# The first mixer's conditioning rows taken by TensorE's column quarters instead of VectorE

## The reference, cut to what matters

```
c_act = jax.nn.silu(c)
for l in range(DEPTH):
    mod = (c_act @ w_mod[l] + b_mod[l])[:, None, :]
    sh1, sc1, g1, sh2, sc2, g2 = jnp.split(mod, 6, axis=-1)
    h = x * (1.0 + sc1) + sh1
    y = hybrid_mixer(h, w_in[l], w_a2[l], b_a[l], gla_norm_g[l], w_out[l])
    ...
```

## Time and profile before

| | |
|---|---|
| median of 3 runs | 1253.62 us (1253.2 to 1255.18) |
| the profiled execution, its own time | 1260.17 us |
| its span in the trace | 1258.4 us |
| PE busy | 1157.7 us (92%) |
| DVE busy | 546.1 us (43%) |
| ACT busy | 284.2 us (23%) |
| moved by DMA | 422.69 MB, mean 336 GB/s |

### The profile page before, as it was taken

How to read it: one execution, slowest core, us unless ns; L and a number is a source line. 1 busy time by engine, 2 the same in 40 slices (tenths; PEclk the granted TensorE clock), 3 DMA queues, 4 the chain that set the end, 5 groups by cost and what they waited for, 6 DMA issues and landing times.

```text
span 1258.4 us, 25820 instructions
## 1 busy us (share of the span) xinstructions
PE 1157.7 (92%) x11004; PEld 637.1 (51%) x11004; DVE 546.1 (43%) x881; ACT 284.2 (23%) x486; POOL 62.1 (5%) x118
## 2 busy tenths in 40 slices
PE   1889679999998897799999999999999999999986
PEld 1779668778878797642333333333333333333322
DVE  6799688867767997732110110121111101210124
ACT  0556234344335654211010010010100100100100
POOL 2101100000012011010000000000000000000101
PEclk9999889999999998899999999999999999999988
DMA  9976696799855865998999999999999999999991
GB/s 342 302 254 203 224 321 221 288 336 382 277 172 159 291 220 194 382 378 315 413 412 399 410 403 407 412 396 411 411 392 412 413 389 411 412 401 411 412 390 55
DMA packets 156504, 422.69 MB, mean 336 GB/s; under 512 B 20988, under 2 KB 74656, under 8 KB 145120
## 3 DMA queue, kind: packets, MB, share of 16 engines
q1 hardware_dynamic: 146720, 395.16, 82.9%
q0 software_dynamic: 6080, 20.31, 4.6%
q10 hardware_dynamic: 3584, 5.51, 1.3%
HBM read 405.20 MB, written 15.73 MB: 334 GB/s over the span
## 4 chain that ended last, share of the span: by engine, by line
PE 66%; DMA 15%; DVE 9%; SPq 4%; issue 3%; ACT 2%; POOL 1%; DVEq 0%; ACTq 0%
PE bank L1376 33%; PE bank L1390 18%; DMA slots<-zeros 8%; PE bank L340 4%; PE bank L342 3%; PE bank L341 3%; DMA raw_w<-in_moe_w_down_dram 3%; DVE mod_acc L1543 2%; DMA raw_u<-in_ffn_w_up_dram 2%; DMA u_raw<-in_w_in_dram 2%; DVE u_low L1554 2%; PE bank L1264 1%; SPq L427 1%; SPq L379 1%; SPq L487 1%
## 5 line engine op out<-in xcount | busy, mean ns | idle before, releaser
L1376 PE MATMUL bank<-raw_w,xg 128*32 128x512 f32 (+1 forms) x4608 | 461.9, 560 | 5.0 <-DMA raw_w<-in_moe_w_up_dram 3.0
L1376 PEld LDWEIGHTS bank<-raw_w,xg 128*32 128x32 f32 x4608 | 154.4, 110 | 309.4 <-issue 301.9
L1928 DVE TENSOR_TENSOR he<-he,bank 128x256 f32<-128x256 f32 (+1 forms) x72 | 25.7, 383 | 535.6 <-ACT he L901 535.6
L1390 PE MATMUL bank<-raw_w,heT 128*32 128x512 f32 x2112 | 232.9, 596 | 3.0 <-DMA raw_w<-in_moe_w_down_dram 2.9
L1390 PEld LDWEIGHTS bank<-raw_w,heT 128*32 128x32 f32 x2112 | 72.0, 110 | 157.8 <-issue 152.9
L901 ACT ACTIVATE he<-bank 128x256 f32<-128x256 f32 (+1 forms) x72 | 21.3, 367 | 572.9 <-PE bank L1376 572.9
L1543 DVE SCALAR_TENSOR_TENSOR mod_acc<-mod_row,c_act,mod_acc 128x1024 f32<-128x1024 f32 x70 | 89.8, 1283 | 7.7 <-DMA mod_row<-in_w_mod_dram 1.5
L340 PE MATMUL bank<-u_high,hT_H 128*128 128x256 f32 x256 | 75.5, 295 | 2.3 <-DVE u_low L1554 2.3
L341 PE MATMUL bank<-u_low,hT_H 128*128 128x256 f32 x256 | 72.7, 284 | 0.0
L342 PE MATMUL bank<-u_high,hT_L 128*128 128x256 f32 x256 | 72.6, 284 | 0.0
L340 PE MATMUL bank<-gu_H,hT_H 128*128 128x512 f32 x160 | 64.8, 405 | 0.0
(11 more groups left out here) (299 smaller groups left out, 1267.0 us busy)
## 6 DMA issues: line engine op xcount, KB each, us to landing
raw_w<-in_moe_w_down_dram SPq DMA_DIRECT2D x88, 1024.0 KB, 16.8
raw_w<-in_moe_w_gate_dram SPq DMA_DIRECT2D x128, 512.0 KB, 13.1
raw_w<-in_moe_w_up_dram SPq DMA_DIRECT2D x128, 512.0 KB, 15.6
mod_row<-in_w_mod_dram SPq DMA_DIRECT2D x80, 512.0 KB, 6.2
raw_w<-in_moe_w_gate_dram SPq DMA_DIRECT2D x64, 384.0 KB, 11.7
raw_w<-in_moe_w_up_dram SPq DMA_DIRECT2D x64, 384.0 KB, 13.5
u_raw<-in_w_in_dram SPq DMA_DIRECT2D x20, 1024.0 KB, 8.2
raw_d<-in_ffn_w_down_dram SPq DMA_DIRECT2D x11, 1024.0 KB, 9.9
```

Of the source, the lines that this page charges most:

```text
L1376: last = mm(bank[g][32 * q:32 * q + 32, 0:2 * HALF[c]].rearrange("s (m j r) -> s m j r", m=2, r=64), xg[:, i, g, k, :], cols[:, :, :, 64 * ...
L1390: last = mm(bank[3 + g][32 * q:32 * q + 32, :], heT[(par + c) % 2][:, g, 2 * a + b, :], W[:, b, h * 512:(h + 1) * 512], start=(c == 0 and ...
L1928: V.tensor_tensor(h, h, bank[g][:, w:2 * w].rearrange("s (j c b) -> s j b c", b=2, c=32), ALU.mult).then_inc(s["m_hid"], 1)
```

## The change

The eight-step accumulation on DVE goes. ACT makes `c_wide`, where each of the 8 values of `silu(c)` on a partition stands 32 times side by side. For each tile PE makes two products: `c_wide[:, k]` (128 x 32) is the stationary side, one half of the tile (512 columns) the moving side, and the result goes to 32 partitions of a bank, one of the four column quarters: 0 and 1 for even k, 2 and 3 for odd k. Bank 4 holds a = 0, bank 5 a = 1. When the eight tiles of an a are through, ACT copies the bank to `ycat[:, a, 0:512]`, and PE turns it to columns as before with 8 x 4 one-column products, now against `half_of`, which picks one row of each of the two quarters that hold a half. Both rounds come after the last tile. The transposes of `stage2` and the tokens come after the tile at place 9, the two halves of the tokens are loaded after the places 5 and 7, and POOL waits for `mod_ps` where it waited for the second `mod_sum`.

```diff
-X_AFTER = (9, 11)
+X_AFTER = (5, 7)
+TOKENS_AFTER = 9
...
+        c_wide = place("c_wide", [P, KT, 32], at=over + 64 * 1024)
...
-            pool.wait_ge(s["mod_sum"], 2)
+            pool.wait_ge(s["mod_ps"], 1)
             gate_bias(0, 2, g_row)
...
             A(c_act[:], c_col[:], ACT.Silu).then_inc(s["cact"], 1)
+            A(c_wide[:], c_col[:].unsqueeze(2).broadcast_to([P, KT, 32]), ACT.Silu).then_inc(s["cwide"], 1)
+            for i, a in enumerate((1, 0)):
+                act.wait_ge(s["rows_ps"], i + 1)
+                A(ycat[:, a, 0:512], bank[4 + a][:], ACT.Copy).then_inc(s["mod_sum"], 1)
...
-            pe.wait_ge(s["mod_sum"], 1)
-            sum_chunk(ycat[:, 1, :], bank[6][:, KT:2 * KT])
-            pe.wait_ge(s["cols_rd"], 1)
-            pe.wait_ge(s["stage2_ld"], 32)
-            nc.tensor.transpose(bank[7][:, 0:P], stage2[:], ident[:]).then_inc(s["stageT"], 1)
-            pe.wait_ge(s["x_ld"], 32)
-            transposed_tokens(x_sb, "xT_ps")
-            pe.wait_ge(s["mod_sum"], 2)
-            sum_chunk(ycat[:, 0, :], bank[6][:, 0:KT]).then_inc(s["mod_ps"], 1)
+            pe.wait_ge(s["cwide"], 1)
+            for i, (a, k) in enumerate(FIRST_ROWS):
+                pe.wait_ge(mod_ld[i], 16)
+                for h in range(2):
+                    p, first = 32 * (2 * (k % 2) + h), a * D + h * 512
+                    last = mm(bank[4 + a][p:p + 32, :], c_wide[:, k, :], mod_first[:, k, first:first + 512], start=(k < 2), stop=(k >= KT - 2))
+                if k == KT - 1:
+                    last.then_inc(s["rows_ps"], 1)
+                if i == TOKENS_AFTER:
+                    pe.wait_ge(s["cols_rd"], 1)
+                    pe.wait_ge(s["stage2_ld"], 32)
+                    nc.tensor.transpose(bank[7][:, 0:P], stage2[:], ident[:]).then_inc(s["stageT"], 1)
+                    pe.wait_ge(s["x_ld"], 32)
+                    transposed_tokens(x_sb, "xT_ps")
+            pe.wait_ge(s["half"], 1)
+            for i, a in enumerate((1, 0)):
+                pe.wait_ge(s["mod_sum"], i + 1)
+                for j in range(KT):
+                    last = mm4(bank[6][:, a * KT + j:a * KT + j + 1], ycat[:, a, j % 4 * P:j % 4 * P + P], half_of[:, j // 4:j // 4 + 1],
+                               start=True, stop=True)
+            last.then_inc(s["mod_ps"], 1)
...
+            dve.wait_ge(s["const"], 1)
+            V.tensor_tensor(half_of[:], ident[:, 0:64:32], ident[:, 64:P:32], ALU.add).then_inc(s["half"], 1)
+            dve.wait_ge(s["stageT"], 1)
+            V.tensor_copy(cols[:], bank[7][:, 0:P]).then_inc(s["cols_rd"], 1)
             dve.wait_ge(s["cact"], 1)
-            before = [0, 0]
-            for i, (a, k) in enumerate(FIRST_ROWS):
-                dve.wait_ge(mod_ld[i], 16)
-                w, acc = mod_first[:, k, a * D:(a + 1) * D], ycat[:, a, :]
-                if k == 0:
-                    last = V.tensor_scalar(acc, w, c_act[:, 0:1], None, ALU.mult)
-                else:
-                    dve.wait_ge(s["dve_chain"], before[a])
-                    last = V.scalar_tensor_tensor(out=acc, in0=w, scalar=c_act[:, k:k + 1], in1=acc,
-                                                  op0=ALU.mult, op1=ALU.add)
...
```

More of the change, by code:

```diff
@@ L300, in hybrid_decoder @@
         s = {}
-        for name in """const c_ld x_ld stage_ld stage2_ld small_ld rows_ld wa2_ld pads stageT cols_rd cact mod_sum ik row_rd mod_ps modT x_ln xT_ps hfull hT_H hT_L
+        for name in """const c_ld x_ld stage_ld stage2_ld small_ld rows_ld wa2_ld pads stageT cols_rd cact cwide half rows_ps mod_sum ik row_rd mod_ps modT x_ln xT_ps hfull hT_H hT_L
             brow_ld gn_ld wH wL proj evac idx_ps relu idxacc dve_chain act_chain pool_chain z_ps az decay
@@ L1459, in conditioning @@
                                               in1=cols[:, c0:c0 + 8], op0=ALU.add, op1=ALU.add)
+            dve.wait_ge(s["const"], 1)
+            V.tensor_tensor(half_of[:], ident[:, 0:64:32], ident[:, 64:P:32], ALU.add).then_inc(s["half"], 1)
+            dve.wait_ge(s["stageT"], 1)
+            V.tensor_copy(cols[:], bank[7][:, 0:P]).then_inc(s["cols_rd"], 1)
             dve.wait_ge(s["cact"], 1)
-            before = [0, 0]
-            for i, (a, k) in enumerate(FIRST_ROWS):
-                dve.wait_ge(mod_ld[i], 16)
-                w, acc = mod_first[:, k, a * D:(a + 1) * D], ycat[:, a, :]
-                if k == 0:
-                    last = V.tensor_scalar(acc, w, c_act[:, 0:1], None, ALU.mult)
-                else:
-                    dve.wait_ge(s["dve_chain"], before[a])
-                    last = V.scalar_tensor_tensor(out=acc, in0=w, scalar=c_act[:, k:k + 1], in1=acc,
-                                                  op0=ALU.mult, op1=ALU.add)
-                if k == KT - 1:
-                    last.then_inc(s["mod_sum"], 1)
-                else:
-                    last.then_inc(s["dve_chain"], 1)
-                    n[0] += 1
-                    before[a] = n[0]
-                if i == 8:
-                    dve.wait_ge(s["stageT"], 1)
-                    V.tensor_copy(cols[:], bank[7][:, 0:P]).then_inc(s["cols_rd"], 1)
             dve.wait_ge(s["cols_rd"], 1)
```

1 line of the change is left out of this document (added).

## The result

The changed kernel takes **1260.18 us** (median of 5 runs, 1259.43 to 1263.2) against 1253.2 us for the kernel before in the same session (5 runs, 1250.3 to 1255.18). The ratio is 1.0064, with a 95% interval of 1.0037 to 1.009. The forecast was 1253.2 us, in a range up to 1256.2. So the change makes the kernel some 7 us slower, and the prediction failed.

The account below looks back on a forecast made before the run. The prediction took load landings, unit 3's and then row 3's, to bound the front, not DVE. Zero for DVE, PE, transposes and IQ1 and -0.4 us for POOL took 1253.62 to 1253.2 us, range 1250.1 to 1256.2.

Parts of the forecast that it names:

- DVE's passes hide behind unit 3's landing: First conditioning: removing DVE's 16 passes gains 0, since modulated tokens are ready 3.2 us before ACT takes them.
- PE's products on two quarters: First conditioning: each tile's two products overlap and take 0.87 us, within the 1.34 us between tiles.
- rival C: First conditioning: the two quarters don't overlap, PE becomes the bound, `modT` at 40.6; 1257.6 us, chance 0.16.
- The transposes: PE behind tile 9: 0.3 us for `stage2` and 3.63 for the tokens, caught up before the last tile; 0.
- BQ: PE's 16 products after the front: all at 2.4 GHz, 7.1 us instead of 10.14, so unit 4 issued near 40.5.
- IQ1 no earlier, row 3's wait gone instead of grown: Loads before `dec`: IQ1 lands at 46.7 instead of 49.24, DVE's row 3 wait grows from 0.86 to 1.7; gain nothing.
- the prediction's last sentence: Wrong if unit 3 lands over a microsecond from 43.6, or lands there and DVE isn't waiting for row 3.
- POOL's 0.4 us for unit 3: POOL's broadcast rows start 1.4 us later, leaving DMA room, so unit 3 lands 0.4 us earlier; bounds 0 and 3.5.
- 0 for DVE, PE, transposes and IQ1: The sum over the front: these four terms add nothing, leaving only POOL's -0.4 us.

Follow-up runs that it names:

- c0_before: The kernel before, unchanged, run and profiled once more: 1252.94 us.
- g set: POOL's clearing transfers moved behind `rms`: kernel before 1274.22 us, with 32 idle products in front 1277.28; changed kernel 1281.24, with 20 in front 1279.55.
- h_b_x_pad52: The kernel before with the change's new places of the token loads alone, and 52 idle products at the start of PE's program: 1249.96 us, 0.998.
- after: The changed kernel's first profile, against the kernel before: median 1260.18 us, ratio 1.0064; the profiled execution is the one of 1259.43 us.
- e_a_again: The changed kernel, unchanged, run and profiled once more: 1260.86 us, 1.0043 of the kernel before.
- b_pad32: The kernel before with 32 idle one-column products (128 instructions) at the start of PE's program: 1261.72 us, ratio 1.007.

## Why the prediction was wrong, step by step

- **That DVE's passes hide behind unit 3's landing: right.** The removed 19 us moved `modT` by 0.3 us at most (32.6 forecast, 32.41 measured, 32.09 before; in the second traces 31.91 and 32.08, so that the direction isn't shown).
- **PE's products on two quarters: right in kind, and overlapping.** The pair of products of a tile (x4, two records to a product) took 1.05 us, where 0.87 was taken and rival C wanted 1.74. The last pair started at 29.77, forecast 29.3.
- **The transposes were priced too high**, 3.63 us against 1.91: the row of before was taken as it stood, though PE had done little ahead of it there. 227 ns for one against 119 is nearly the ratio of the two levels, 1.2 and 2.4 GHz, although the granted clock reads 1.00 in both traces.
- **BQ was priced too low**, 7.1 us against 8.83. Three windows of BQ in the changed kernel, in the columns of the earlier trace rows:

```profile
33.30:34.30 1.00, 0.93 (x4) 0.75 (x5) 1.00 (x3) 0.00 (x0) 0.71 (x3) 0.98 1.13 343
34.30:37.70 3.40, 3.40 (x9) 2.75 (x9) 2.10 (x5) 0.23 (x1) 3.40 (x7) 0.50 1.07 382
37.70:42.20 4.50, 4.50 (x25) 3.68 (x27) 1.84 (x2) 3.58 (x3) 0.94 (x2) 1.00 1.06 389
```

  The granted clock went to 0.50, that is 1.2 GHz, for 3.4 us, although PE had been busy for most of the time before and had waited only 1.14 us for `hfull`. I had reasoned that a busy PE keeps the upper level; here it didn't. Unit 4 was issued at 42.24, forecast 40.5.
- **IQ1 no earlier, row 3's wait gone instead of grown: wrong, without weight.** With IQ1 landing at 49.69 and not at 46.7, DVE waits 2.19 us for its high part, takes its low part, and row 3 has landed by then; `dec` starts at 56.43 and the chain goes on level. By the prediction's last sentence this alone makes it wrong: unit 3 landed within a microsecond of 43.6, and row 3 isn't what DVE waits for.
- **POOL's 0.4 us for unit 3: not shown.** POOL starts its rows at 32.56 (forecast 32.6), and unit 3 lands 1.07 us earlier, at 42.93 (forecast 43.6). But with POOL as it was, unit 3 lands at 43.24 in `c0_before` and at 40.77 to 43.67 in before's padded kernels, so the 1.07 us can't be put down to POOL. By `dec` nothing is left of it.
- **The step that failed** is in the sum: "0 for DVE, PE, transposes and IQ1". It counted what PE's added instructions do in the front and took the rest of the program as unmoved. The runs showed that 128 added instructions that do nothing make the kernel before 1.007 times as long, and that the same kernel is 0.9988 with 208 of them and 1.0003 with 256 at the end of the program. The front was rightly costed at nothing; the price shows from 130 us on. For the stalls it is shown that the added instructions make them by what they displace; for the stretch up to 480 us it isn't.
- **No rival had it.** C came out near the time (1257.6) by a mechanism that the trace refutes. The range of 1250.1 to 1256.2 was built from costs in the front only.

Shown is that the stalls behind PE's jumps come and go with the loop's position, in both kernels; that padding alone gives the whole loss at position 178; and that length and the loads' places cost nothing that can be measured. Open is the part that no stall explains: 1.0021 to 1.0067 in the changed kernels without stalls, where before's timed ones lie at 0.998 to 1.0024. At equal positions it is about 0.3% to 0.4% at 2 and 4 (1.0021 and 1.0024 against 0.998 to 0.9993) more at 52 against 50 (1.0059 against 1.0 to 1.0024), and nothing at 178 and 180, where the g set has 4.0 us, which is within its intervals. As far as single traces tell, it lies between 130 and 480 us, where the last `rms` waits for a chain of transfers of uneven length; whether it is the position of the straight code there, or the times at which the engines come into it, these runs don't separate. No version beat the kernel before beyond its interval; the nearest, `h_b_x_pad52`, is 0.998 [0.9959, 1.0001].

## What to carry to other kernels

If an edit adds or removes instructions on an engine that has a counted loop later in its program, count how far the loop moves in blocks of 256 instructions, and look in the waits behind the jumps back for time with nothing to wait for. A change of half a per cent in a kernel with such a loop should not be put down to the edited lines before the same number of idle instructions has been tried in the old kernel. And where two profiled spans agree but the medians don't, compare stretches between fixed events, not the ends.

## What the runs showed of the hardware

- A jump back of PE showed no stall at six of the nine positions tried, 2.0 to 2.3 us at position 146 and 3.3 to 3.6 us, with 0.67 more ahead of it, at 178 and 180. In the long case 14 or 15 records (7 products) run first and then the engine stands still.
- Kernels with stalled jumps fetched 92 packets of 16 KB on the queue for instructions, those without 89 or 90.
- Behind the first such stall the granted clock fell (0.72 over the 6 us that follow), behind the second it stayed at 1.00 in `after` and `e_a_again` and fell to the same 0.72 in `b_pad32`. Where it fell, 177 records took 21.20 us instead of 19.50, so a short stall can cost PE more than its length.
- A chain of eight transfers of POOL, each issued when the one before had landed, took 31.0 to 38.0 us from its first to its last issue in the second mixer of sixteen traces of kernels that have the chain at the same place.
- Time lost at the jumps was in part given back near 1200 us, where the kernel before waits for weights. Lag of the same DVE instruction in `b_pad32` behind `c0_before`, at its time in `c0_before`:

```
 561.72 us   6.79
 756.33 us  13.49
 926.34 us  19.94
1236.03 us   9.55
```

  6.7 and 6.5 us were lost at the two jumps, and 10.4 us came back.
- The same 16 transposes took 1.91 us where PE had worked on every tile ahead of them, and 3.63 us where it had been idle for 13.84 us until shortly before.
